# A two-layer hybrid trunk on one core: attention steps gathered into fewer pieces between the projections, and the order of scores, maxima and last gelus

## The reference, cut to what matters

```python
for l in range(DEPTH):                                   # 2 layers, x is (1, 512, 1024)
    z = rms_norm(x, pre_mix_g[l]) @ w_in[l]              # 1024 -> u 512 | v 512 | q 512 | k 512 | values 512
    u, v_g = gelu(z[u]), gelu(z[v])
    y_a = u * (tril_chunks(ws) @ layer_norm(v_g) + bias) # 4 groups of 128 channels, blocks of 128 positions
    q, k = rope(z[q]) * 64 ** -0.5, rope(z[k])           # 4 heads, two softmaxes of width 64 each
    a = softmax(q0 k0) - lam * softmax(q1 k1)            # chunk-causal, by blocks of 128 queries
    y_b = rms_norm(a @ values, subln_g[l]) * (1 - lam_init)
    x = x + rms_norm(concat(y_a, y_b) @ w_out[l], post_mix_g[l])
    h = rms_norm(x, pre_ffn_g[l])
    x = x + rms_norm((silu(h @ w_gate) * (h @ w_up)) @ w_down, post_ffn_g[l])
```

## Time and profile before

| | |
|---|---|
| median of 3 runs | 1085.51 us (1085.47 to 1085.52) |
| the profiled execution | 1085.77 us, of which the span is 1083.6 us |
| PE busy | 1076.2 us, 99% of the span |
| DVE, ACT, POOL busy | 613.3, 586.1, 579.5 us (57%, 54%, 53%) |
| granted clock of PE | 9 tenths or more in all 40 slices of the page |

### The profile page before, as it was taken

One profiled execution on the slowest core, in us unless ns is written; L12 is line 12 of the kernel. 1 busy time (PEld: TensorE's weight loads), 2 busy tenths in 40 slices (PEclk: granted clock), 3 DMA queues, 4 the chain that ended last, 5 costly groups with the idle time before them and its releaser, 6 DMA issues.

```text
span 1083.6 us, 17591 instructions
## 1 busy us (share of the span) xinstructions
PE 1076.2 (99%) x6836; PEld 968.3 (89%) x6836; DVE 613.3 (57%) x1011; ACT 586.1 (54%) x1143; POOL 579.5 (53%) x450
## 2 busy tenths in 40 slices
PE   9999999999999999999999999999999999999997
PEld 7888788999999999888888888889999999988886
DVE  4376554888888884010344756458888888820103
ACT  6767784666555554221457568655665555531212
POOL 3534364567666665544444344655766666654440
PEclk9999999999999999999999999999999999999999
DMA  9423212424433434523253222232443343263212
GB/s 293 144 60 102 73 59 80 154 79 118 117 99 98 118 103 164 181 97 97 86 161 104 78 79 78 75 127 72 118 117 98 97 117 106 92 223 114 96 53 77
DMA packets 145335, 119.37 MB, mean 110 GB/s; under 512 B 3802, under 2 KB 120036, under 8 KB 145252
## 3 DMA queue, kind: packets, MB, share of 16 engines
q1 hardware_dynamic: 145236, 118.24, 34.9%
q10 hardware_dynamic: 16, 0.00, 0.0%
HBM read 111.94 MB, written 6.29 MB: 109 GB/s over the span
## 4 chain that ended last, share of the span: by engine, by line
PE 99%; ACT 0%; DMA 0%; DVE 0%; issue 0%; DVEq 0%; ACTq 0%
PE banks L603 30%; PE banks L605 30%; PE banks L604 30%; PE banks L668 2%; PE banks L696 2%; PE banks L612 1%; PE banks L681 1%; PE banks L873 1%; PE banks L707 1%; DMA x_rows<-in_x_dram 0%; PE banks L714 0%; ACT junk L1084 0%; PE banks L958 0%; DVE scratch L1500 0%; DVE x_rows L1534 0%
## 5 line engine op out<-in xcount | busy, mean ns | idle before, releaser
L534 POOL TENSOR_TENSOR w_lo<-raw,w_hi 128x512 fp32r<-128x512 f32 x204 | 264.7, 1322 | 292.2 <-ACT w_hi L1076 292.2
L552 POOL TENSOR_TENSOR w_lo<-raw,w_hi 128x512 fp32r<-128x512 f32 x200 | 261.2, 1316 | 141.1 <-ACT w_hi L1145 136.7
L603 PE MATMUL banks<-xg_hi,w_hi 128*128 128x256 f32 (+1 forms) x896 | 276.3, 308 | 0.0
L605 PE MATMUL banks<-xg_lo,w_hi 128*128 128x256 f32 (+1 forms) x896 | 274.2, 306 | 0.0
L604 PE MATMUL banks<-xg_hi,w_lo 128*128 128x256 f32 (+1 forms) x896 | 274.0, 306 | 0.0
L1076 ACT ACTIVATE w_hi<-raw 128x1024 fp32r<-128x1024 f32 x102 | 107.1, 1061 | 161.4 <-PE banks L605 151.5
L1145 ACT ACTIVATE w_hi<-raw 128x512 fp32r<-128x512 f32 x200 | 125.1, 630 | 114.9 <-DVE raw L1785 61.3
L605 PEld LDWEIGHTS banks<-xg_lo,w_hi 128*128 128x128 f32 x896 | 171.2, 191 | 7.8
L603 PEld LDWEIGHTS banks<-xg_hi,w_hi 128*128 128x128 f32 x896 | 171.2, 191 | 7.6
L604 PEld LDWEIGHTS banks<-xg_hi,w_lo 128*128 128x128 f32 x896 | 171.3, 191 | 6.9
L603 PE MATMUL banks<-w_hi,hid_hi 128*128 128x512 f32 x352 | 137.2, 390 | 0.0
(11 more groups left out here) (180 smaller groups left out, 1889.8 us busy)
## 6 DMA issues: line engine op xcount, KB each, us to landing
raw<-in_w_gate_up_dram SPq DMA_DIRECT2D x88, 512.0 KB, 4.1
raw<-in_w_down_dram SPq DMA_DIRECT2D x44, 512.0 KB, 3.5
raw<-in_w_in_dram SPq DMA_DIRECT2D x40, 512.0 KB, 3.7
raw<-in_w_out_dram SPq DMA_DIRECT2D x16, 512.0 KB, 3.5
x_spill<-x_rows SPq DMA_DIRECT2D x8, 512.0 KB, 4.9
x_rows<-x_spill SPq DMA_DIRECT2D x8, 512.0 KB, 5.1
x_rows<-in_x_dram SPq DMA_DIRECT2D x4, 512.0 KB, 7.2
out_dram<-x_rows SPq DMA_DIRECT2D x8, 256.0 KB, 2.0
```

The costliest lines, as they stand in the source:

```text
L534: last = tt(lo[:, piece], raw_half(l, c, h)[:, piece], hi[:, piece].bitcast(F32), ALU.subtract)
L552: tt(lo, full, hi.bitcast(F32), ALU.subtract).then_inc(w_ready, 1)
L603: mm(o, stat[0], mov[0], start=first, stop=False)
L605: return mm(o, stat[0], mov[1], start=False, stop=last)
```

## The change

Four things are changed together, in all engines' orders. (1) Scores of i = 0 and i = 1 now share banks 2 and 3, side by side; i = 2 uses banks 2 and 3, i = 3 banks 4 and 5 (`SC_AT`). With that `maxima`, `exponentials` and `combine` of a step with i = 0 wait until the scores, maxima and exponentials of the next step are there too. (2) `turn` of i = 3 uses bank 4 (`T_BANKS_OF`), and turns, weighs and gates that stood apart between projections stand together. (3) The gates of groups 0 to 2 move ahead of `qk_half(5)`, the fourth behind `scores_of_two(8)`, and `add_terms` on DVE with them. (4) At the end of the mixer `copy_u(3)` and the last two gelus stand ahead of two turned copies and `take_heads(6)` on ACT, and heads 0 to 2 are turned in one piece on PE.

```diff
     T_BANKS = {T1: 2, T2: 3}
-    SC_BANKS = [(2, 3), (4, 5)]
-    T_BANK, O_BANK = 6, 7
-    GATE_BANKS = [2, 3, 4, 5]
+    SC_AT = [(2, 0), (2, 256), (2, 0), (4, 0)]
+    T_BANKS_OF = [6, 6, 6, 4]
+    O_BANK = 7
+    GATE_BANKS = [2, 3, 5, 5]
     QK_TILES = [(K0, 0), (Q0, 0), (K0, 1), (Q0, 1), (K0, 2), (Q0, 2), (K0, 3), (Q0, 3)]
     QK_BANKS = [4, 5, 6, 7, 0, 1, 0, 1]
...
                     pe.wait_ge(qk_ready, 8 * l + 2 * h + 2)
                 if n == 0:
                     pe.wait_ge(vg_gelu, ST * l + 4)
-                elif n == 8 or n == 9:
-                    pe.wait_ge(gm_added, G * l + 2 * (n - 7))
-                elif n > 1:
+                elif i == 0:
                     pe.wait_ge(a_ready, NS * l + n - 1)
+                elif i == 2:
+                    pe.wait_ge(a_ready, NS * l + n)
+                elif i == 3 and h > 0:
+                    pe.wait_ge(a_ready, NS * l + n - 3)
+                    pe.wait_ge(at_copied, NS * l + n - 3)
+                if h == 2 and i == 0:
+                    pe.wait_ge(gm_added, G * l + 2)
+                elif h == 2 and i == 3:
+                    pe.wait_ge(gm_added, G * l + 4)
                 w = max(w, 2 * P)
+                b, at = SC_AT[i]
                 for n_pass, (q, k) in enumerate(((q_rot, k_rot), (q_low, k_rot), (q_rot, k_low))):
                     for j in range(2):
                         ps = slice(j * HD, (j + 1) * HD)
-                        last = mm(bank[SC_BANKS[n % 2][j]][:, 0:w], q[ps, h, i * P:(i + 1) * P], k[ps, h, 0:w],
+                        last = mm(bank[b + j][:, at:at + w], q[ps, h, i * P:(i + 1) * P], k[ps, h, 0:w],
                                   start=(n_pass == 0), stop=(n_pass == 2))
...
                 pe.wait_ge(a_ready, NS * l + n + 1)
+                i = n % ST
                 if n == 0:
                     pe.wait_ge(qk_ready, 8 * l + 3)
-                elif n % ST != 1:
+                elif i == 0:
+                    pe.wait_ge(at_copied, NS * l + n - 1)
+                elif i == 2:
                     pe.wait_ge(at_copied, NS * l + n)
...
                     pe.wait_ge(va_copied, ST * l + 2 * m + 2)
                 if m == 0:
                     pe.wait_ge(ws_copied, l + 1)
-                else:
+                elif m != 2:
                     pe.wait_ge(o_taken, 8 * l + m)
...
                     for k in range(i + 1):
-                        last = mm(bank[O_BANK][:, (n % 2) * P:(n % 2 + 1) * P], attn_t(n, k),
+                        last = mm(b_tr[O_BANK][:, n % ST, :], attn_t(n, k),
                                   v_att[:, k, h * P:(h + 1) * P], start=(k == 0), stop=(k == i))
                 last.then_inc(pv_ready, 1)
...
                     pe.wait_ge(ws_masked, l + 1)
                     pe.wait_ge(xhat_ready, ST * l + ST)
-                pe.wait_ge(a_ready, NS * l + (7 if g < 2 else 8))
+                if g < 3:
+                    pe.wait_ge(a_ready, NS * l + (7 if g < 2 else 8))
+                else:
+                    pe.wait_ge(gm_added, G * l + 3)
                 for n in range(ST):
                     last = mm(b_tr[GATE_BANKS[g]][:, n, :], v_gate[:, n, g * P:(g + 1) * P], wsT[:, g, :],
                               start=True, stop=True)
...
                 turn_two(0)
                 va(C_VA, 1, (0, 1))
                 va(C_VA + 1, 0, (0, 1))
-                turn(l, 2)
                 va(C_VA + 1, 1, (0, 1))
-                turn(l, 3)
+                turn_two(2)
                 pe.wait_ge(qk_ready, 8 * l + 4)
                 pe.wait_ge(tables_landed, 16 * 5 * (l + 1))
...
                 weigh(l, 0)
                 va(C_VA + 1, 1, (2, 3))
                 qk_half(l, 4, lower)
-                turn(l, 6)
+                qk_half(l, 4, upper)
+                turn_two(6)
                 weigh(l, 1)
-                qk_half(l, 4, upper)
-                turn(l, 7)
                 weigh(l, 2)
+                for g in range(3):
+                    gate(l, g)
                 qk_half(l, 5, lower)
                 qk_half(l, 5, upper)
-                for g in range(G):
-                    gate(l, g)
-                weigh(l, 3)
                 qk_half(l, 6, lower)
                 qk_half(l, 6, upper)
                 scores_of_two(8)
+                weigh(l, 3)
+                gate(l, 3)
                 qk_half(l, 7, lower)
...
                 u_half(l, 0, upper)
-                turn(l, 10)
+                u_half(l, 1, lower)
+                turn_two(10)
                 weigh(l, 4)
-                u_half(l, 1, lower)
-                turn(l, 11)
                 scores_of_two(12)
                 u_half(l, 1, upper)
                 u_half(l, 2, lower)
...
                 weigh(l, 5)
                 u_half(l, 2, upper)
                 u_half(l, 3, lower)
-                turn(l, 14)
+                u_half(l, 3, upper)
+                turn_two(14)
                 weigh(l, 6)
-                u_half(l, 3, upper)
-                turn(l, 15)
                 out_k(l, 0)
...
                 out_k(l, 2)
-                turn_head(l, 0)
+                for h in range(H - 1):
+                    turn_head(l, h)
                 out_k(l, 3)
-                turn_head(l, 1)
-                turn_head(l, 2)
                 out_k(l, 4)
                 turn_head(l, 3)
                 for k in range(5, KT):
...
                 def exponentials(n):
                     w = (n % ST + 1) * P
-                    act.wait_ge(max_ready, NS * l + n + 1)
+                    act.wait_ge(max_ready, NS * l + n + (2 if n % ST == 0 else 1))
                     if n >= 2:
                         act.wait_ge(a_ready, NS * l + n - 1)
+                    b, at = SC_AT[n % ST]
                     for j in range(2):
-                        o = bank[SC_BANKS[n % 2][j]][:, 0:w]
+                        o = bank[b + j][:, at:at + w]
                         fn(prob[n % 2][:, 0:w] if j == 0 else o, o, ACT.Exp, bias=nmx[:, n, j:j + 1],
                            accum_out=psumr[:, n, j:j + 1]).then_inc(exp_done, 1)
...
-                    act.wait_ge(pv_ready, 8 * l + m + 1)
+                    act.wait_ge(pv_ready, 8 * l + m + (2 if m == 1 else 1))
...
                 copy_turned(1)
                 exponentials(3)
                 rotated_high(3)
-                copy_turned(2)
                 copy_values(0)
                 copy_values(1)
+                copy_turned(2)
                 copy_turned(3)
                 act.wait_ge(ws_turned, l + 1)
                 fn(wsT[:, :, :], b_tr[O_BANK][:, :, :], ACT.Copy).then_inc(ws_copied, 1)
...
                 take_heads(0)
                 high(l, 7, 0)
                 high(l, 7, 1)
+                swapped(4)
                 copy_turned(6)
+                copy_turned(7)
                 take_heads(1)
-                swapped(4)
-                copy_turned(7)
                 take_heads(2)
...
                 rotated_high(5)
-                take_heads(3)
                 swapped(6)
                 exponentials(8)
                 exponentials(9)
+                take_heads(3)
                 rotated_high(6)
                 high(l, 9, 0)
                 swapped(7)
...
                 exponentials(11)
                 high(l, 9, 1)
                 copy_u(0)
+                high(l, 10, 0)
                 copy_turned(10)
+                copy_turned(11)
                 take_heads(4)
-                high(l, 10, 0)
-                copy_turned(11)
                 exponentials(12)
                 exponentials(13)
                 copy_u(1)
...
                 high(l, 11, 0)
                 gated_high(0)
                 gated_high(1)
-                copy_turned(14)
-                take_heads(6)
                 copy_u(3)
-                copy_turned(15)
                 u_gelus(2)
                 u_gelus(3)
+                copy_turned(14)
+                copy_turned(15)
+                take_heads(6)
                 head_roots(0, 0, H - 1)
...
                 head_roots(1, H - 1, H)
+                high(l, 12, 0)
                 head_high(0)
-                high(l, 12, 0)
                 head_high(1)
                 head_high(2)
                 high(l, 12, 1)
...
                         .then_inc(qk_ready, 1)
                 def maxima(n):
-                    b, w = SC_BANKS[n % 2][0], (n % ST + 1) * P
-                    dve.wait_ge(sc_ready, NS * l + n + 1)
-                    nc.vector.memset(banks[0:CH, b:b + 2, w - CH:w], NEG_INF).then_inc(sc_masked, 1)
+                    b, at = SC_AT[n % ST]
+                    to = at + (n % ST + 1) * P
+                    dve.wait_ge(sc_ready, NS * l + n + (2 if n % ST == 0 else 1))
+                    nc.vector.memset(banks[0:CH, b:b + 2, to - CH:to], NEG_INF).then_inc(sc_masked, 1)
                     dve.wait_ge(sc_masked, NS * l + n + 1)
```

(34 more changed lines are left out.)

## The result

The changed kernel takes **1099.49 us** (median of 4 runs, 1098.58 to 1101.31), the kernel before beside it 1085.49 (1085.42 to 1085.52): a ratio of 1.0131 [1.0116, 1.0146]. It is 14.0 us slower, where 7.8 had been forecast, and it lies 3.0 us above the range.

What follows compares the result with a forecast made beforehand. PE was taken to bound both mixers, busy throughout. Per layer 1.6 + 0.6 + 1.8 − 0.1 = 3.9, in both 7.8 us, giving 1093.3 us; range 1089.5 to 1096.5.

Steps and rivals of the forecast that it cites:

- Gathering: Pieces between PE's products fall from 19 to 13 a layer, gaining 0.1 us a layer, 0.2 us in both.
- The two rivals that needed met waits: Waits met, only gathering counts: 1085.3 us, 8 in 100; interruptions cost more, passing 1083.3 us: 3 in 100.
- the three named waits: PE waits before qk_half(4), before scores(8) and before the turned heads: 1.6, 0.6 and 1.8 us a layer.
- the one in which wait 3 alone vanishes: Rival: the twelve scalings take 2.4 us, done before PE wants them; other waits stand; 1089.7 us, 12 in 100.
- The fourth, in which further waits fail: Rival: the close waits fail too, each later wait pushing the next; 1096 to 1099 us, 7 in 100.
- Wait 1: Before qk_half(4): PE stands for copy_values(2), 1.6 us a layer, bounds 0.9 and 1.9.
- Wait 2: Before scores(8): PE arrives before rotated_low(5) is ready, 0.6 us a layer, bounds 0.3 and 0.8.
- Wait 3: Before the turned heads: scalings end after PE wants head 2, 1.8 us a layer, bounds 1.2 and 2.1.
- C: Start of ACT's copy_u(3); head 2 was forecast wanted at C + 11.9, scalings done at C + 13.7.
- POOL's work beside it hangs on the same root, so that the length stays: Step for the turned heads: scaling of heads 0 to 2 starts 0.6 behind the root and keeps its 6.66 us.
- waits add to the end: Everything downstream is paced by PE, so each PE wait adds to the kernel's time.
- The rule drawn from the Trainium skill: DVE instructions with two SBUF inputs and GpSimd ones reading SBUF lock shared ports; used for the wait before qk_half(4): 1.6 to 1.9.

Runs made afterwards that it cites:

- experiment 10: Changed kernel with the mixer's end as before, copy_values(2) ahead of exponentials(6) and weigh(3) ahead of qk_half(6): 1085.48 us, ratio 0.9998.
- experiments 8 to 10: Changed kernel, mixer's end as before, with copy_values(2) ahead of exponentials(6): 1086.54 us; with weigh(3) ahead of qk_half(6): 1088.45 us; with both: 1085.48 us.
- experiment 1: Changed kernel with one ACT instruction put back, high(12, 0) behind head_high(0) again: 1093.16 us, ratio 1.0069.
- experiment 4: Kernel before, with only heads 0 to 2 turned in one piece and high(12, 0) ahead of head_high(0): 1094.79 us, ratio 1.0082.
- experiment 7: Changed kernel with 24 unused transposes on PE between head 0 and head 1 in each layer: 1097.27 us, ratio 1.0106.
- Experiment 6: Changed kernel with POOL's low(12, 0) held until DVE has scaled the first three heads, ACT's order kept: 1093.22 us, ratio 1.0068.

## Why the prediction was right in kind and wrong in size

- **Gathering, 0.1 us a layer.** Not contradicted, and tested for half of it: with every wait gone the kernel is level with before (experiment 10), but only three of the six pieces a layer are saved there. The two rivals that needed met waits fall, since the three named waits all came, and with them the one in which wait 3 alone vanishes. The fourth, in which further waits fail, comes near the time but not by its mechanism: no wait at scores(2), u_half(1) or scores(14) stands in the view of waits.
- **Wait 1, put at 1.6 us.** Measured 1.38 in the timeline and 1.5 by experiments 8 to 10. (Its lower bound of 0.9 left out the 0.1 for starting again, which the sum itself counts.) The steps came as worked out: the view of DVE's timeline has normalize_gate(0) at 77.70 (put at 77.9) and its four operations in 6.25 us (put at 6.4), the first slowed by POOL only in part.

```profile
77.70 1.16 DVE L1636 SCALAR_TENSOR_TENSOR v_gate<-v_gate,mv,ln_rows 128x512 f32<-128x512 f32 x1
78.89 1.67 DVE L1638 SCALAR_TENSOR_TENSOR v_gate<-v_gate,ln_rs,ln_rows 128x512 f32<-128x512 f32 x1
...
83.95 0.17 DVE L1614 MEMSET banks<- 64x128 f32 x1
```

- **Wait 2, put at 0.6 us.** Measured 0.60, and 0.53 to 0.54 by the experiments.
- **Wait 3, put at 1.8 us.** Measured 3.8. PE wanted head 2 as worked out, at about 161.6, which is C + 11.9 and the 0.55 already lost before out_k(2); but the scalings ended at C + 15.7, where 13.7 had been put. The step that failed is "POOL's work beside it hangs on the same root, so that the length stays". It does hang on the root up to low(11, 1). What follows on POOL, low(12, 0), hung in the kernel before on high(12, 0) behind head_high(0), and so on PE having turned head 0; the change cut that tie. Two more of POOL's subtractions then ran beside the scalings, and these took 8.67 us instead of 6.66. The move stood in the diff, and the prediction named no price for it. With the move undone the wait is what was forecast: 0.55 before out_k(2) and, from experiment 1, 0.9 and 0.3 at the heads, 1.75 us, and the whole kernel is then at 1093.16 where 1093.3 had been forecast for all of the change.
- **The clock**, not in the prediction. This is the second step that failed: it let a wait cost its own length and no more ("waits add to the end"). With a stand of 2.8 us PE's granted clock fell to 0.50, in both layers of both profiled kernels that have such a stand (the changed one and experiment 4's); with stands of 0.7 to 1.2 us it did not. By experiment 7 this is 2.2 us of the median.

The sum with the measured waits, and the forecast's 0.1 for gathering, is 2 × (1.38 + 0.60 + 3.8 − 0.1) = 11.4, so 1085.5 + 11.4 = 1096.9 with the clock left at full speed. Experiment 7, which has just that, took 1097.27; 0.15 of the 0.4 between them is the time of before, which was 1085.65 beside it, and the rest is not traced. What is left up to the 1099.5 measured, 2.2 us, is what filling the wait gave back: the clock.

The rule drawn from the Trainium skill (SBUF — State Buffer, "Who interferes with whom") went further than the prediction took it. The same section counts tensor_scalar among the operations that can, under conditions on their operands, take the ports shared with GpSimd, and says of such an operation and a GpSimd instruction that the later one blocks until the other is through. The scalings are tensor_scalar operations, and the trace agrees: 0.2 us from start to start alone, about 1.24 beside POOL's subtractions, which start about 1.25 apart; one long scaling for every subtraction, six here and four before. Experiment 6 shows that the overlap is the cause; that it is the ports was not tried apart.

## What to carry to other kernels

When a duration is taken over from a trace, ask what set it: twelve scalings took 6.66 us because POOL was busy beside four of them, and a move on a third engine made it six. For each instruction that is moved earlier, follow what it lets go on the other engines, and what that runs beside. And a wait on the bounding engine is to be priced with its clock: here the long one, once in each of the two layers, cost 2.2 us more than its own length at the median. Filling it with unused work gave that back, and in the kernel where it was 0.8 us the clock stayed up.

## What the chip showed that was not expected

- The half clock that comes with the long wait differs from layer to layer, 3.4 and 6.8 us for the same stand, and from one execution to the next. The four runs of the changed kernel lie from 1098.58 to 1101.31 with mean granted clocks of 0.998 down to 0.995 over the whole span, in step with their spans (1096.5 to 1099.2); with the wait filled they lie within 0.13 us. A spread that is new after a change can itself be a sign that the clock falls. The mean clock alone is no measure of the loss: one execution of the kernel before showed 0.948 over its span and took 1086.38 us, 0.7 more than the median beside it; its trace was not kept.
- Unused work on the bounding engine made the kernel faster: 24 transposes in each layer, 2.2 us less.
- No cost of interrupting the stream of products could be told: three pieces fewer a layer, with the waits away (experiment 10), gave 0.14 us in both layers together. The interval of that run leaves room for about 0.2 us a piece, so this is no proof that an interruption is free.
